# Regrouping the side work of a two-block transformer kernel: more halts per group, earlier first products of two inverses, GpSimd scaling RWKV's projections

## The reference, cut to what matters

```python
def first_block(x, ...):
    n = rmsnorm(x, attn_norm[l]); u = n @ w_in[l]          # 2048 -> 7696 columns
    u_gdn, u_mlstm, u_rglru, u_rwkv = jnp.split(u, MIXER_SPLITS, axis=-1)
    ...                                                     # four mixers of width 512
    x = x + mix @ w_out[l]
    n = rmsnorm(x, ffn_norm[l])
    x = x + (silu(n @ ffn_w_gate[l]) * (n @ ffn_w_up[l])) @ ffn_w_down[l]
    return rmsnorm(x, final_norm)

def mlstm(u, conv_w, b_i, b_f, norm_w):
    qk, v, o_raw, i_raw, f_raw = jnp.split(u, [2 * W, 3 * W, 4 * W, 4 * W + H], axis=-1)
    qk = jax.nn.silu(causal_conv(qk, conv_w))               # four taps over the tokens
    ...
def rwkv7_time_mix(u, mu, ...):
    u_prev = jnp.pad(u, ((0, 0), (1, 0), (0, 0)))[:, :-1]
    u = u + (u_prev - u) * mu                               # "shift" in the kernel
    ...                                                     # a scan, in chunks of 64 in the kernel
def gated_delta_rule(q, k, v, g, beta):                     # chunkwise, with a triangular inverse
    sol = lax.linalg.triangular_solve(lower + eye, rhs, left_side=True, lower=True, unit_diagonal=True)
```

## Time and profile before

| | before |
|---|---|
| median of 3 runs | 2499.42 us (2498.58 to 2499.59) |
| the profiled execution | 2499.0 us, its span 2497.1 us |
| PE busy | 2428.7 us (97%) |
| DVE busy | 1425.2 us (57%) |
| ACT busy | 1127.7 us (45%) |
| POOL busy | 104.0 us (4%) |
| mean granted TensorE clock | 0.990 of full |

### The profile page before, as it was taken

One profiled execution on the slowest core, in us unless ns is written; L12 is line 12 of the kernel. 1 busy time (PEld: TensorE's weight loads), 2 busy tenths in 40 slices (PEclk: granted clock), 3 DMA queues, 4 the chain that ended last, 5 costly groups with the idle time before them and its releaser, 6 DMA issues. The chain is left out here.

```text
span 2497.1 us, 34280 instructions
## 1 busy us (share of the span) xinstructions
PE 2428.7 (97%) x14448; PEld 2067.1 (83%) x14448; DVE 1425.2 (57%) x1845; ACT 1127.7 (45%) x1401; POOL 104.0 (4%) x93
## 2 busy tenths in 40 slices
PE   7999899989999999999999999999999999999998
PEld 6997889977788888888888878898888888888887
DVE  4666665667574555555555575544446555545554
ACT  5634434554354444344444464455544455344444
POOL 2000000130000000000000031000000000000000
PEclk9999999999999999999999999999999999999999
DMA  7533324644456555555555547555545544565564
GB/s 235 199 123 109 128 95 144 227 153 170 135 199 198 185 186 185 194 191 187 185 186 185 186 161 260 185 171 174 173 158 169 192 147 151 185 202 185 185 240 148
DMA packets 225642, 441.53 MB, mean 177 GB/s; under 512 B 11891, under 2 KB 28113, under 8 KB 223057
## 3 DMA queue, kind: packets, MB, share of 16 engines
q1 hardware_dynamic: 221744, 419.80, 51.2%
q0 software_dynamic: 3744, 19.53, 2.1%
HBM read 428.81 MB, written 10.49 MB: 176 GB/s over the span
## 5 line engine op out<-in xcount | busy, mean ns | idle before, releaser
L1203 ACT CAST ringH<-raw 128x1024 fp32r<-128x1024 f32 x780 | 816.3, 1049 | 1080.7 <-PE ps L594 888.9
L1758 DVE TENSOR_TENSOR ringL<-raw,ringH 128x1024 fp32r<-128x1024 f32 x780 | 954.9, 1241 | 441.2 <-ACT ringH L1203 439.9
L592 PE MATMUL ps<-ringH,nS 128*128 128x512 f32 x1376 | 554.9, 403 | 5.1 <-DVE ringL L1758 3.9
L593 PE MATMUL ps<-ringL,nS 128*128 128x512 f32 x1376 | 539.6, 392 | 0.0
L594 PE MATMUL ps<-ringH,nS 128*128 128x512 f32 x1376 | 539.5, 392 | 0.0
L620 PE MATMUL ps<-nS,ringH 128*128 128x256 f32 x1056 | 312.9, 296 | 13.9 <-DVE ringL L1758 12.0
L592 PEld LDWEIGHTS ps<-ringH,nS 128*128 128x128 f32 x1376 | 260.6, 189 | 60.1 <-issue 5.0
L594 PEld LDWEIGHTS ps<-ringH,nS 128*128 128x128 f32 x1376 | 260.1, 189 | 56.0
L593 PEld LDWEIGHTS ps<-ringL,nS 128*128 128x128 f32 x1376 | 261.0, 190 | 49.8 <-issue 0.2
L621 PE MATMUL ps<-nS,ringH 128*128 128x256 f32 x1056 | 302.1, 286 | 0.0
L622 PE MATMUL ps<-nS,ringL 128*128 128x256 f32 x1056 | 301.9, 286 | 0.0
(11 more groups left out here) (398 smaller groups left out, 2147.5 us busy)
## 6 DMA issues: line engine op xcount, KB each, us to landing
raw<-in_w_in SPq DMA_DIRECT2D x189, 1024.0 KB, 5.1
raw<-in_ffn_w_gate SPq DMA_DIRECT2D x44, 1024.0 KB, 5.2
raw<-in_ffn_w_up SPq DMA_DIRECT2D x44, 1024.0 KB, 5.2
raw<-in_ffn_w_down SPq DMA_DIRECT2D x44, 1024.0 KB, 5.1
raw<-in_w_out SPq DMA_DIRECT2D x32, 1024.0 KB, 5.1
raw<-in_w_mem_kv SPq DMA_DIRECT2D x16, 1024.0 KB, 5.2
raw<-in_w_proj_a SPq DMA_DIRECT2D x8, 1024.0 KB, 5.1
raw<-in_w_proj_m SPq DMA_DIRECT2D x8, 1024.0 KB, 5.4
```

The costliest lines, as they stand in the source:

```text
L592: mm(o, XH[:, ts(j)], WH, first, False)
L593: mm(o, XH[:, ts(j)], WL, False, False)
L1203: e.copy(ringH[:, h % NSPL, 0:nh * cols], raw[:, u % NRAW, h0 * cols:(h0 + nh) * cols]).then_inc(*hi.tick(h))
L1758: tt2(ringL[:, h % NSPL, o], raw[:, u % NRAW, h0 * cols:(h0 + nh) * cols], ringH[:, h % NSPL, o].bitcast(F32), SUB).then_inc(*lo.tick(h))
```

## The change

- **Norm.** ScalarE's two sums of squares move from between the transposed rows to behind them; three halts of pace 2 are added before the norm factor's transpose on TensorE. VectorE copies a `w` block from PSUM unscaled, and GpSimd multiplies it by `rxb` later; RWKV's `shift` now waits for GpSimd. The four steps that stood between the parameters' loads and their transpose are gone. GpSimd's norm and params stages become one, `begin`.
- **Gates.** The halt of pace 6 becomes two of 3, with VectorE's wait for the logarithm behind the new one; ScalarE's `Exp` of `a_log` comes ahead of the `Ln`.
- **mLSTM.** The stage starts once `m0` is done instead of `m3`, waits for `m1` and `m3` by halting, and has one group of the convolution per halt instead of two.
- **Inverses.** The first blocks are made by a new function `pairs` right after the triangle: in `rwkv` behind `NT`, in `gdn` behind the second half of `G8`.
- **GDN.** A halt of pace 9 becomes two of 5, with one more on every engine; between the state's product (KS) and the next "vn" stands a new halt of 3.5, and the halts of 5.5 become 4.5; ScalarE squares for the output norm before it does z's Silu.
- **RG-LRU.** One group of the convolution per halt, with one more halt on each engine per half.
- **Statistics.** `stat2` gets three halts of one step each on TensorE, and halts inside on ScalarE and VectorE.

```diff
-    while not L.done("m3"):
+    while not L.done("m0"):
...
-    L.step(4)
...
-    L.run("stat2")
+    L.weave(L.stage("stat2"), 2)
...
+                for _ in range(3):
+                    yield 2
                 factor("nx", nx_p, nx_v, rx)
                 yield 1
...
-                yield 6
+                yield 3
+                yield 3
...
-                    L.upto(f"m{q}")
-                    yield
-                    yield
-                L.upto("m3")
+                    while not L.done(f"m{q}"):
+                        yield
+                    for _ in range(4):
+                        yield
+                while not L.done("m3"):
+                    yield
                 yield
...
-                yield 9
+                yield 5
+                yield 5
...
                             t = m1(b[:, ts(h)], K[:, h, 128:256], Sx[:, h, :], h == 0)
                         t.then_inc(*gd_p.tick("KS"))
+                        yield 3.5
                     b = take("gd", "vn", ch)
                     e.wait_ge(*gd_v.at("R", ch))
                     for h in range(4):
                         t = m1(b[:, ts(h)], XR8[:, 2 * h + ch, :], R[:, h, :], h == 0)
                     t.then_inc(*gd_p.tick("vn", ch))
-                    yield 5.5
+                    yield 4.5
...
                             t = m1(b[:, ts(h)], Kt[:, h, :], VN[0][:, h, :], h == 0)
                         t.then_inc(*gd_p.tick("S"))
-                        yield 5.5
+                        yield 4.5
...
+            def stat2(L):
+                for _ in range(3):
+                    yield 1
...
+                square = squared(nx_a, xtok, small[:, 112:114], s_x, v2(MU + 988, 2048))
                 yield from to_rows("nx", nx_p, nx_a, lambda k: g0[:, k:k + 1], lambda k: nS[:, k, 0, :], lambda n: None,
-                                   squared(nx_a, xtok, small[:, 112:114], s_x, v2(MU + 988, 2048)), (5, 6))
+                                   square, ())
+                square(0)
+                yield
+                square(1)
+                yield
+                yield
                 root(nx_v, nx_a, rx)
                 yield
...
                 act(gc, gc, ACT.Exp, scale=-1.0).then_inc(*gt_a.tick())
+                e.wait_ge(s_p, 16 * (len(PARAMS) - 2 + 4))
+                act(small[:, 2:3], small[:, 1:2], ACT.Exp).then_inc(*gt_a.tick("al"))
                 e.wait_ge(s_c, 48)
                 e.wait_ge(*gt_a.now())
                 act(gc, gc, ACT.Ln, bias=csg[:, 2:3]).then_inc(*gt_a.tick("ln"))
-                e.wait_ge(s_p, 16 * (len(PARAMS) - 2 + 4))
-                act(small[:, 2:3], small[:, 1:2], ACT.Exp).then_inc(*gt_a.tick("al"))
+                yield
                 yield
                 yield
...
                         e.wait_ge(*mv.at(*name, k))
                         act(dst[:, k, :], dst[:, k, :], ACT.Silu).then_inc(*ma.tick(*name, k))
-                    if k % 2:
+                    if k % per == per - 1:
                         yield
...
                 e.wait_ge(*gd_v.at("dt0"))
                 act(DT, DT, ACT.Exp).then_inc(*gd_a.tick("D"))
+                yield
                 kd, eG = small[:, 32:36], small[:, 36:40]
                 e.wait_ge(*gd_v.at("kd0"))
                 act(kd, kd, ACT.Exp).then_inc(*gd_a.tick("kd"))
...
                 L.upto("g3")
+                e.wait_ge(*gd_v.at("O", 1))
+                head_norm(("gdnrm",), [(u4(2)[:, k:k + 2, :], v3(SC + 5120, 4, T)[:, k:k + 2, :]) for k in (0, 2)], col_rw, gd_a, gd_v)
                 e.wait_ge(*pool.at("g3"))
                 act(mix[:, 0:4, :], mix[:, 0:4, :], ACT.Silu).then_inc(*gd_a.tick("z"))
-                e.wait_ge(*gd_v.at("O", 1))
-                head_norm(("gdnrm",), [(u4(2)[:, k:k + 2, :], v3(SC + 5120, 4, T)[:, k:k + 2, :]) for k in (0, 2)], col_rw, gd_a, gd_v)
...
             def stat2(L):
                 square_roots(st_v, st_a, ("x2",), r1)
+                yield
                 square_roots(st_v, st_a, ("x2b",), r2)
                 yield
...
-                        e.wait_ge(*nx_v.at("rb"))
-                        tt2(wU[:, k:k + 2, 1:], ps, bc(rxb, 2), MUL).then_inc(*drain_v.tick(tag))
+                        e.tensor_copy(wU[:, k:k + 2, 1:], ps).then_inc(*drain_v.tick(tag))
...
+                if key == "nx":
+                    yield
...
+                for _ in range(2):
+                    yield
+                yield from factor("nx", nx_p, nx_a, nx_v, 112, rxb)
...
+                yield
                 e.wait_ge(*gt_a.at("ln"))
...
+            def pairs(key, mv, of, GT, XTr):
+
                 if of is wide:
                     first = [(s, bc(mask(C_M1T), 4), bc(ident, 4)) for s in (slice(0, 4), slice(4, 8))]
                 else:
@@ -1966,6 +1994,8 @@
                 for s, pairs, one in first:
                     own(mv)
                     tt2(XTr[:, s, :], one, XTr[:, s, :], SUB).then_inc(*mv.tick(*((*key, "xt", -1) if s.stop == 8 else ())))
+
+            def invert(key, mp, mv, of, X, XTr, T1, levels):
                 yield
...
-                    e.wait_ge(*drain_v.at(f"w{k // 4 + 4 * (k % 4 == 2)}"))
+                    e.wait_ge(*pool.at(f"w{k // 4 + 4 * (k % 4 == 2)}"))
                     tt2(to, wU[:, k:k + 2, 0:T], wU[:, k:k + 2, 1:], SUB).then_inc(*rw_v.tick())
...
                     within("N", NT, 1.0)
+                    own(rw_v)
+                    pairs((hh, "inv"), rw_v, narrow, GT, XR)
                     yield
                     product("RK", RK, C_BSI, 1.0)
                     yield
                     NV = v3(SC + 512 * 6, 8, 64)
                     yield
                     own(rw_v)
-                    yield from invert((hh, "inv"), rw_p, rw_v, narrow, GT, X, XR, T1, 5)
...
-                    L.upto(f"m{q}")
-                    yield from conv(mU[:, 4 * q:4 * q + 4, :], 4, "mlstm_conv", 8, 4 * q, (Q, K)[q], ml_a, ml_v, ("cv", q))
-                L.upto("m3")
+                    while not L.done(f"m{q}"):
+                        yield
+                    yield from conv(mU[:, 4 * q:4 * q + 4, :], 4, "mlstm_conv", 8, 4 * q, (Q, K)[q], ml_a, ml_v, ("cv", q), 1)
+                while not L.done("m3"):
...
+                        if w == 0 and g == 1:
+                            own(gd_v)
+                            pairs(("inv",), gd_v, wide, G8, XR8)
...
+                if s.last and tag[0] == "w":
+                    q = int(tag[1])
+                    k = 4 * q if q < 4 else 4 * (q - 4) + 2
+                    e.wait_ge(*drain_v.at(tag))
+                    e.wait_ge(*nx_v.at("rb"))
+                    e.tensor_tensor(wU[:, k:k + 2, 1:], wU[:, k:k + 2, 1:], bc(rxb, 2), MUL).then_inc(*pool.tick(tag))
...
-                for _ in range(5):
+                for _ in range(6):
```

More of the change, by code:

```diff
@@ L1180, in tensor @@
             course(lane(unit, {
-                "norm": norm, "turn": turn_params, "gates": gates, "mem": mem, "rwkv": rwkv, "mlstm": mlstm, "gdn": gdn,
+                "norm": norm, "turn": turn_params, "gates": gates, "stat2": stat2, "mem": mem, "rwkv": rwkv, "mlstm": mlstm, "gdn": gdn,
                 "rglru": rglru, "mix312": split(12), "mix0": split(4), **{f"split1.{q}": split1(q) for q in range(4)},
@@ L1597, in rglru @@
                         e.wait_ge(*rg_v.at(0, "end"))
-                    yield from conv(L, "r0", rU[:, s2, :], 2, "rglru_conv", 2 * hf, X, rg_a, rg_v, ("cv", hf), False)
+                    yield from conv(L, "r0", rU[:, s2, :], 2, "rglru_conv", 2 * hf, X, rg_a, rg_v, ("cv", hf), False, 1)
                     for q, (dst, nm) in enumerate(((Rr, "rglru_b_a"), (Ii, "rglru_b_x"))):
@@ L1900, in norm @@
                 yield from to_rows("nx", nx_a, nx_v, lambda k: g0[:, k:k + 1], lambda k: (nS[:, k, 0, :], nS[:, k, 1, :]))
-                factor("nx", nx_p, nx_a, nx_v, 112, rxb)
+                for _ in range(2):
+                    yield
+                yield from factor("nx", nx_p, nx_a, nx_v, 112, rxb)
                 yield
@@ L1955, in mem @@
                 yield
-                factor("me", me_p, me_a, me_v, 116, rmb)
+                yield from factor("me", me_p, me_a, me_v, 116, rmb)
                 yield
-            def invert(key, mp, mv, of, GT, X, XTr, T1, levels):
+            def pairs(key, mv, of, GT, XTr):
                 if of is wide:
@@ L2118, in rwkv @@
                     own(rw_v)
-                    yield from invert((hh, "inv"), rw_p, rw_v, narrow, GT, X, XR, T1, 5)
+                    yield from invert((hh, "inv"), rw_p, rw_v, narrow, X, XR, T1, 5)
                     product("RB", RBv, C_BSI, 1.0)
@@ L2402, in rglru @@
                     s2 = slice(2 * hf, 2 * hf + 2)
-                    yield from conv(rU[:, s2, :], 2, "rglru_conv", 4, 2 * hf, X, rg_a, rg_v, ("cv", hf))
+                    yield from conv(rU[:, s2, :], 2, "rglru_conv", 4, 2 * hf, X, rg_a, rg_v, ("cv", hf), 1)
                     e.wait_ge(*rg_a.at(hf, "g", 1))
```

(16 more changed lines are left out.)

20 lines of the change are left out of this document (13 added, 7 removed).

## The result

The changed kernel takes 2481.99 us (median of 4 runs, 2480.23 to 2486.87) against 2499.51 us (4 runs, 2498.58 to 2501.34): a ratio of 0.9932, 95% interval 0.9915 to 0.9949, so 17.5 us or 0.7% faster. The forecast was 2474 us, 25 us faster; the measured time lies inside its range.

What follows compares the result with a forecast made beforehand. TensorE bounds the kernel, busy 2428.7 of 2497.1 us, with few long waits and half clock behind them. Gains 45.1 less costs 15.7 give 29.4 us; with 4 kept back, 25 us off 2499.0: 2474 us, range 2459 to 2491.

Steps and rivals of the forecast that it cites:

- GDN, right side, output norm: GDN: waits for decay matrix and first blocks go, 12.6 us; longer halt, 4.1; Silu behind squares, 3.8.
- rival C: GDN: GpSimd's decay matrix stays late, the 10 us stay and 12.6 us of gain go: 2487 us; chance 0.09.
- Norm: Norm factor: TensorE's 3.0 us wait falls to 1.5; with 1.4 of clock, 2.9 us gained.
- Gates: Gates: low halves emitted ahead of the wait for the logarithm; 3.7 plus 1.3 us, 5.0 gained.
- GpSimd's scaling of w: Norm's w blocks: shift waits some 1.3 us for GpSimd, but TensorE needs the sigmoid later; cost taken as 0.
- mLSTM from m0: RWKV's second half: first-block wait goes, gain 9.8 us; new waits on X, mask, state, heads and clock cost 15.7.
- Statistics: Statistics near 1493.91 us: halts let low halves into VectorE's chain; 3.91 us wait and 3.0 of clock, 6.9 gained.
- the reserve: 4 us left in seven places that will not all come out to nothing, about 0.6 each.
- B: GpSimd's seven scalings block VectorE and are paid in full, 9.0 us on top: 2483 us; chance 0.10.
- A: The early mLSTM convolution groups are free, costing TensorE nothing: 2458 us; chance 0.13.
- D: No change: the waits go but come back for the weights: 2499 us; chance 0.07.
- E: Slower: from the first early convolution on, close waits in RWKV keep the clock at half: 2534 us; chance 0.06.

Runs made afterwards that it cites:

- run 2: The changed kernel with GpSimd's seven scalings of w cut to one column of each row: 2482.56 us, ratio 0.9936.
- run 5: The changed kernel with the memory's work held back for two halts of RWKV (tanh and sigmoid; the keys' squares): 2474.14 us, ratio 0.9894.
- run 4: The changed kernel with mLSTM begun at `m3` again, two convolutions to a halt, `pairs` still early: 2480.85 us, ratio 0.9926.
- run 6: The changed kernel with mLSTM's convolutions of `m0` and `m1` begun two halts later on every engine: 2475.83 us, ratio 0.9905.
- run 7: The changed kernel with the statistics' halts paced 2, 1, 1 instead of 1, 1, 1: 2485.04 us, ratio 0.9935.
- run 10: The kernel before with only the change's GDN and RG-LRU halts, right side, Silu behind the squares and GDN's early `pairs`: 2479.34 us, ratio 0.9919.
- run 3: The changed kernel with GpSimd's products beside GDN's last convolutions (decay matrix, gate, rows of `kv0`) cut to one column: 2478.93 us, ratio 0.9922.
- run 11: The changed kernel with `pairs` of all three inverses at the start of the inverse again: 2487.07 us, ratio 0.9957.
- run 12: The changed kernel with memory rows held back, convolutions two halts later, and `kv0` scaled behind GDN's decay matrix: 2465.84 us, ratio 0.9866.
- Kernel 9: The changed kernel with memory rows held back and mLSTM's convolutions two halts later, statistics left as changed: 2466.92 us, ratio 0.9867.

## Why the prediction was right, and where it was not

The direction, the size class and the main mechanism were right. By its own steps:

- **GDN, right side, output norm** (12.6 + 4.1 + 3.8 = 20.5 us): measured alone 19.5. VectorE's 10 us behind GpSimd's matrix are gone (0.3 us are left) and rival C with them. What stayed is 3.1 us for low halves.
- **Norm** (new wait 1.5): 1.5. **Gates** (5.0): the 3.7 us are gone; 0.8 us for a row of the gates is new, so some 4.2.
- **GpSimd's scaling of w** (0, with "TensorE needs the sigmoid only ten steps later" as cover): 0, by run 2. The cover itself was wrong, as the next point shows; it only wasn't needed for the scaling.
- **The step that failed is one that the sum doesn't have.** It priced the longer norm at its own wait and left out what the eight w-steps more ahead of `mem` (twelve added, four taken away) push along: the memory's rows slide two halts further into RWKV, one ahead of tanh and sigmoid, one ahead of the squares. That costs 6.9 - 3.0 = 3.9 us of waits and 1.2 + 1.4 of clock in the traces, 6.5 together; run 5 takes the memory out of the way and gives back 7.8 by its median, 4.0 by its profiled span.
- **mLSTM from m0** (gain 9.8, cost 15.7): named rightly, each wait within 0.5 us: X 1.2 forecast, 1.7 found; mask 2.2 and 2.2; state 4.2 and 3.9. Too high were the 0.5 one level on and the 1.4 in `m1`'s next halt (no wait found), the heads (2.0 forecast, 0.4 found) and the clock (4.2 against 1.6 + 1.3 in the stretches at 181 and 218 us). X was 0.5 above and the state 0.3 below its forecast, so the cost came out 4.6 us lower. So the part as a whole is near -1 and not -5.9: run 4 differs by 1 us. Run 6 shows that the waits come from standing behind GpSimd's scaling.
- **`pairs`** carried more than the 1.8 us put down for RWKV: 2.4 there, and 4.5 in GDN, where the prediction had it in one sum with the rest.
- **Statistics** (6.9, bounds 4 and 6.9): mis-sized. 0.8 us of waits and 1.7 of clock came, 2.5. Low halves do get in, but the chain's table and the rotation of `qa0` are VectorE's as well, and only their sum counts (run 7).
- **The sum.** 29.4 forecast before the reserve, less 1.0 (GDN), 0.8 (gates), 6.5 (start of RWKV) and 4.4 (statistics), plus 4.6 (mLSTM), is 21.3 us; the profiled executions differ by 18.7. Of the 2.6 us between, 1.7 are clock in no term: stretches at 327 to 333 and 464 to 470 us in the changed kernel (PEclk 0.72 over 6 us, 1.7 each), less one of 1.7 at 192 to 198 before. The rest stays unplaced; two executions of one kernel differ by more, as the last section shows. The reserve of 4 us was meant for such small waits and was no match for the one place that the sum lacked.
- **What was luck.** The parts outside GDN were to bring 29.4 - 20.5 = 8.9 us, or 4.9 with the whole reserve taken from them; they brought about -2 (run 10). The direction held because GDN's part did. And the cost of mLSTM, put 4.6 us too high, made up for most of the 6.5 us that the sum lacked at the start of RWKV.
- **Rivals.** B is right about the mechanism and wrong about its price: a GpSimd product blocks VectorE nearly in full (run 3), but of seven scalings and five products TensorE feels 1.4 us. A is out (the early groups cost 3.9 + 2.2 + 1.7 us of waits; its figure, 2458, lies just outside the range that is said to take in most of it). D is out: the interval of the ratio ends at 0.9949, and no wait for a transfer of weights is in the list. E is out (no stretch at half clock in the changed kernel lasts over 5 us), but the row that spoke against it was read short: it covers 552 to 557 us only, and the clock stays at half from the end of the wait at 551.76 to 558, PEclk 0.50 over 6.2 us. GDN's clock term was thus 3.1 us and not 2.5.

The rest of the changed kernel's deficit to 2467 us is settled by runs 5, 6 and 9. Open is whether `pairs` in GDN could stand where it delays neither the first blocks nor the low half at 535 us (run 11 shows either one or the other), and whether less work for VectorE in the statistics' chain would pay: neither was tried.

## What to carry to other kernels

When work is spread over more halts, list what else advances by the same halts: a stage that comes later slides into its neighbour's tightest place, and its rows there may cost more than the halts brought. A shift of two halts was worth 7.8 us here, and one of two halts for the convolutions 6.2, each more than a third of what the change brought. Start an early piece of work when its input is ready on the engine that finishes it (GpSimd's scaling), not when its block is complete; an in-order queue makes everything behind it wait too. And before easing one place in a chain of one engine, add up all that the engine must do between two low halves: moving a part of it only moves the wait.

## What the runs showed of the hardware

Beside GpSimd's products of 128x1024 elements (2.41 us), three of VectorE's convolution operations took 4.28 and 6.07 us instead of 1.52, and four scalings of 128x128 with a column were stretched alike: 0.87 us with no GpSimd product beside them (run 3), 2.78 beside one (the changed kernel), 4.94 beside two (run 12). Cutting a GpSimd operation from 128x512 to 128x2 elements took its mean only from 1.55 to 0.55 us, and the one with the mask, cut to 128x8, took 2.56 us in run 3, as long as the full one, while another product of 128x8 took 0.22 us right behind it. No run shows why:

```profile
511.15 2.56 POOL L2681 TENSOR_TENSOR AR<-AR,cm 128x8 f32<-128x8 f32 x1
```

The clock goes with the scatter between executions of one kernel: the four runs of the changed kernel have spans of 2478.4, 2478.7, 2481.6 and 2485.0 us at a mean granted clock of 0.994, 0.994, 0.992 and 0.991. Half the rate also shows up where TensorE had waited little: the changed kernel has it from 327.7 and from 464.3 us on, though TensorE was busy all through the 4.3 us ahead of the second. Kernel 9 has it at neither place, and at 352 to 360 us instead (PEclk 0.57).
